# A one-hot of the expert gates moved from VectorE to ScalarE, in the first dense stage of a PEER layer

## The reference, cut to what matters

```python
sc, ci = lax.top_k(cand, PEER_TOPK)
e1 = jnp.take_along_axis(i1, ci // PEER_TOPK, axis=-1)
e2 = jnp.take_along_axis(i2, ci % PEER_TOPK, axis=-1)
idx = (e1 * N_KEYS + e2).reshape(PEER_BLOCK, PEER_HEADS * PEER_TOPK)
gate = jax.nn.softmax(sc, axis=-1).reshape(PEER_BLOCK, PEER_HEADS * PEER_TOPK)
u = lp['peer_u'][idx]
act = jax.nn.gelu(jnp.einsum('bkd,bd->bk', u, xb).astype(jnp.float32), approximate=False)
return jnp.einsum('bk,bkd->bd', (gate * act).astype(xb.dtype), lp['peer_v'][idx])
```

## Time and profile before

| | |
|---|---|
| time, median of 3 runs | 4661.38 us (4657.36 to 4670.94) |
| the profiled execution's own time | 4685.36 us |
| its span, first to last instruction | 4683.5 us |
| busy, share of the span | PE 77%, DVE 52%, POOL 32%, ACT 20% |
| mean granted clock of TensorE | 0.88 |

### The profile page before, as it was taken

One profiled execution on the slowest core, in us unless ns is written; L12 is line 12 of the kernel. 1 busy time (PEld: TensorE's weight loads), 2 busy tenths in 40 slices (PEclk: granted clock), 3 DMA queues, 4 the chain that ended last, 5 costly groups with the idle time before them and its releaser, 6 DMA issues. The chain is left out here.

```text
span 4683.5 us, 57981 instructions
## 1 busy us (share of the span) xinstructions
PE 3621.7 (77%) x21974; PEld 2555.1 (55%) x21974; DVE 2433.7 (52%) x5117; ACT 926.4 (20%) x1361; POOL 1483.9 (32%) x1266
## 2 busy tenths in 40 slices
PE   8687899985869969677878798764577677678894
PEld 2354576753546859566666575542344445444473
DVE  3055222225214330577879788789566566543354
ACT  1222111111222031122222232211111111111221
POOL 0000111100000112044555354557566566554400
PEclk9898899996979979888989899886788889889996
DMA  5200110111013052277889798788999999999963
GB/s 222 100 28 14 32 31 29 38 34 62 27 67 127 27 172 91 94 251 267 299 319 362 272 363 288 289 305 311 332 354 373 355 369 374 351 355 341 327 170 126
DMA packets 422161, 977.69 MB, mean 209 GB/s; under 512 B 164657, under 2 KB 191481, under 8 KB 417936
## 3 DMA queue, kind: packets, MB, share of 16 engines
q0 software_dynamic: 150912, 549.52, 31.5%
q1 hardware_dynamic: 270992, 424.63, 27.0%
HBM read 861.15 MB, written 112.88 MB: 208 GB/s over the span
## 5 line engine op out<-in xcount | busy, mean ns | idle before, releaser
L1874 POOL DMA_INDIRECT u_rows<-in_u_rows,idx_u x512 | 666.6, 1302 | 932.7 <-DVE dots L1912 687.4
L1885 POOL DMA_INDIRECT v_rows<-in_v,idx_v x512 | 631.9, 1234 | 312.5 <-PE ff_ps L1971 167.4
L1912 DVE CUSTOM_DVE_ANT_0 u_rows<-u_rows,x_rows 128x1024 f32<-128x1024 f32 x512 | 619.6, 1221 | 161.1 <-DMA u_rows<-in_u_rows,idx_u 135.2
L2306 PE MATMUL hid_ps<-dh,u_high 128*128 128x512 f32 x1024 | 427.8, 418 | 93.3 <-DVE u_low L2558 92.9
L2306 PE MATMUL hid_ps<-dl,u_high 128*128 128x512 f32 x1024 | 422.9, 413 | 0.0
L2306 PE MATMUL hid_ps<-dh,u_low 128*128 128x512 f32 x1024 | 420.8, 411 | 0.0
L2723 PE MATMUL turn_ps<-w_high,dh 128*128 128x512 f32 x384 | 170.5, 444 | 290.6 <-DVEq L2775 256.9
L1971 PE MATMUL ff_ps<-v_rows,diag 128*8 128x512 f32 x2048 | 264.9, 638 | 84.9 <-DMA v_rows<-in_v,idx_v 83.8
L2306 PEld LDWEIGHTS hid_ps<-dh,u_high 128*128 128x128 f32 x1024 | 202.6, 198 | 158.6 <-DVE u_low L2558 113.1
L2723 PEld LDWEIGHTS turn_ps<-w_high,dh 128*128 128x128 f32 x384 | 77.4, 201 | 358.4 <-DVEq L2775 204.6
L684 PE MATMUL side_ps_scan<-h,w_side_scan 128*128 128x344 f32 x768 | 269.1, 476 | 0.2
(11 more groups left out here) (407 smaller groups left out, 6780.1 us busy)
## 6 DMA issues: line engine op xcount, KB each, us to landing
u_raw<-in_u SPq DMA_DIRECT2D x128, 512.0 KB, 6.5
v_raw<-in_v SPq DMA_DIRECT2D x128, 512.0 KB, 5.9
hidden_saved<-hid SPq DMA_DIRECT2D x128, 256.0 KB, 5.9
gates_saved<-gates SPq DMA_DIRECT2D x64, 512.0 KB, 6.9
g_back<-gates_saved SPq DMA_DIRECT2D x16, 2048.0 KB, 39.8
hidden_back<-hidden_saved SPq DMA_DIRECT2D x128, 256.0 KB, 5.0
slab<-in_w_ada SPq DMA_DIRECT2D x12, 2048.0 KB
side_saved<-side_scan SPq DMA_DIRECT2D x16, 516.0 KB
```

The source lines that it names most:

```text
L1874: self.nc.gpsimd.indirect_dma_start(self.u[:, n % RU], None, self.io["u_rows"], bass.IndirectOffsetOnAxis(ap=index, axis=axis)).then_inc(l ...
L1885: self.nc.gpsimd.indirect_dma_start(self.v[:, n % RV], None, self.io["v"], bass.IndirectOffsetOnAxis(ap=index, axis=0)).then_inc(self.v_la ...
L1912: V.tensor_tensor_reduce(self.u[:, n % RU], self.u[:, n % RU], self.xt[:], 1.0, 0.0, ALU.mult, ALU.add, accum_out=self.dots[:, i % 2, k:k ...
L2306: mm = nc.tensor.matmul(ps[b % 2][:], u[:, b % 2, k], h[:, k], start=at == 0, stop=at == 3 * KD - 1)
```

## The change

`second` is no longer formed by DVE. ACT forms it: for each of the four tokens of a group one 128 x 128 activation Abs(index - key), with the index as a per-partition bias and scale -1, then, after a wait for its own four results, one 128 x 512 Relu(1 - x) in place, with a column of ones as bias. For integers this is 1 where they are equal and 0 elsewhere. ACT waits, as DVE does, until PE has used the buffer two groups before. The copy of the products out of PSUM becomes a list entry of its own, `take_gates`, placed behind the *next* group's `gates`; the store by SP goes with it. The planner counts a `gates` group as 1.6 in place of 2.3, and `take_gates` as nothing.

```diff
         if not kind.sparse:
-            groups = [("gates", kind.i * NGRP + g) for g in range(NGRP)]
+            groups = [(what, kind.i * NGRP + g - late) for g in range(NGRP + 1)
+                      for what, late in (("gates", 0), ("take_gates", 1)) if 0 <= g - late < NGRP]
...
-        else:
-            now += 2.3
+        elif item[0] == "gates":
+            now += 1.6
             pe += 1.1
...
-                    elif e[0] == "gates" and e[1] % 2 == 1:
+                    elif e[0] == "take_gates" and e[1] % 2 == 1:
                         b = e[1] // 2
                         sp.wait_ge(g_taken, e[1] + 1)
                         sp.dma_start(io["gates"][:, b], gates[:, b % 2]).then_inc(g_stored[b % 2], 16)
...
                         if kind.i >= 2:
-                            act.wait_ge(second_ready, (kind.i - 1) * NGRP)
+                            act.wait_ge(first_ready, (kind.i - 1) * NGRP)
+                            act.wait_ge(away, (kind.i - 1) * P)
...
                     elif e[0] == "gates":
+                        g = e[1]
+                        d = g // NGRP
+                        if g >= 2:
+                            act.wait_ge(g_summed, g - 1)
+                        if g % NGRP == 0:
+                            turn = next(k.m for k in SELECT if not k.sparse and k.i == d)
+                            act.wait_ge(s_taken, fills["turn", turn] + 1)
+                        for t in range(GRP):
+                            at = g % NGRP * GRP + t
+                            S.activation(second[:, g % 2, t], col(consts, "iota"), ACT.Abs, scale=-1.0,
+                                         bias=slots[:, d % 2, 1, at:at + 1]).then_inc(away, 1)
+                        act.wait_ge(away, (g + 1) * GRP)
+                        S.activation(second[:, g % 2], second[:, g % 2], ACT.Relu, scale=-1.0, bias=col(consts, "ones"))\
+                            .then_inc(second_ready, 1)
+                    elif e[0] == "take_gates":
                         g = e[1]
                         b = g // 2
                         act.wait_ge(g_summed, g + 1)
...
                         ins.then_inc(first_ready, 1)
-                        at = g % NGRP * GRP
-                        V.tensor_tensor(second[:, g % 2], iota.unsqueeze(1).to_broadcast([P, GRP, NKEY]),
-                                        slots[:, d % 2, 1, at:at + GRP].unsqueeze(2).to_broadcast([P, GRP, NKEY]),
-                                        ALU.is_equal).then_inc(second_ready, 1)
```

More of the change, by code:

```diff
@@ L2237, in peer_up @@
         (keys_loaded, u0, u1, u_high, u_low, summed, finished, h0, h1, q_loaded, scored, s_taken, read, chain, exp_in,
-         gate_ready, slots_ready, turned, first_ready, second_ready, g_summed, g_taken, g0_stored, g1_stored, up_carried) = sems(
+         gate_ready, slots_ready, turned, first_ready, second_ready, g_summed, g_taken, g0_stored, g1_stored, away, up_carried) = sems(
             ph, "keys_loaded", "u0_loaded", "u1_loaded", "u_high_ready", "u_low_ready", "hid_summed", "hid_finished",
             "hid0_stored", "hid1_stored", "q_loaded", "peer_scored", "s_taken", "s_read", "select_chain", "exp_in", "gate_ready",
-            "slots_ready", "slots_turned", "first_ready", "second_ready", "gates_summed", "gates_taken", "gates0_stored", "gates1_stored",
+            "slots_ready", "slots_turned", "first_ready", "second_ready", "gates_summed", "gates_taken", "gates0_stored", "gates1_stored", "second_away",
             "up_carried")
```

## The result

The changed kernel takes 4686.87 us (median of 8 runs), the one before 4664.48 in the same comparison: a ratio of 1.0049, 95% interval 1.0031 to 1.0067, so 22 us slower. One of the eight executions of the kernel before took 7797 us; without it the median before is 4661.38. The forecast was 17 us slower.

What follows compares the result with a forecast made beforehand. Peer_up was taken as bound mostly by PE, its tail by DVE, peer_down by transfers while gathers run. Peer_up 35 us shorter (44 - 16 + 7) and peer_down 52 longer gave +17: 4678 us on the median, range 4610 to 4725.

Steps and rivals of the forecast that it cites:

- The sum: Whole kernel: peer_up 35 us shorter and peer_down 52 longer, so 17 us slower.
- ACT's price: Gates groups: four Abs, a Relu, a short wait and the copy take 2.47 us of ACT, 79 us per set.
- The sets: Gates of D0 to D2: ACT becomes the pace, 119, 96, 102 us become 93, 90, 90; D3 gains 7.
- The tail: Stretch between the gates of D2 and D3: 13 blocks moved there bring their u_low onto full DVE, 16 us longer.
- peer_down: Second stage: 56 moved gathers add 115 us, dense pairs done beside them save 63 at the end; net 52 longer.
- ACT hidden: Rival, gates sets: ACT under about 1.9 us a group, sets go at PE's pace; 57 us faster, 4604; chance 0.22.
- Taking turns: Rival, gates sets: ACT's copy waits for PE and the next `second` for the copy; 140 us slower, 4801; chance 0.12.
- Table loads: Rival, Gelus among the gates of D0 to D2: two loads more each, 41 us on ACT; 4719; chance 0.04.

Runs made afterwards that it cites:

- e6: The changed kernel with one 128x512 Abs per group in place of four 128x128, three quarters of the one-hots wrong: 4656.35 us, ratio 0.9972.
- e3: The changed kernel with the planner's interval of gathers in peer_up at 2.1 in place of 2.3: 4678.13 us, ratio 1.0024.
- e7: The kernel before with the planner's gates cost at 1.6 and gather interval at 2.1, both one-hots on VectorE: 4663.5 us, ratio 0.9993.
- e1: The changed kernel with the planner's cost of a gates group put back from 1.6 to 2.3: 4689 us, ratio 1.0043.
- e2: The kernel before with the planner's cost of a gates group at 1.6 in place of 2.3, one-hot on VectorE: 4646.56 us, ratio 0.9948.
- e9: The kernel before with only the planner's gates cost at 1.6, measured again on one chip with three others: 4649.86 us, ratio 0.9963.
- e12: The changed kernel itself, measured again on one chip with three others: 4688.7 us, ratio 1.0037.
- e10: The changed kernel, plan and later copy kept, with the second one-hot back on VectorE, measured again on one chip: 4651.71 us, ratio 0.9960.
- e4: The kernel before with only the planner's interval of gathers in peer_up raised from 2.3 to 2.5: 4693.7 us, ratio 1.0054.
- e5: The changed kernel with ScalarE forming the second one-hot of even groups only, VectorE that of odd groups: 4670.06 us, ratio 1.0005.

## Why the prediction was right

**The sum.** Forecast: peer_up 35 us shorter, peer_down 52 longer, +17. Profiles: 47 shorter and 56 longer, with a long profile of before; +22 by the medians.

**ACT's price** was estimated at 0.39 us for an Abs, 0.71 for a Relu and 2.47 for a group: 0.390, 0.723 and 2.40. The nearest row, an activation with the same kind of operand, gave it to 3%. That ACT would be the pace of the gates sets was right for D1 to D3, 91 to 96% busy: e6 shows it, for nothing but ACT's work was shortened there. For D0, 84% busy, it was wrong, as e6 shows too.

**The sets.** Forecast 93, 90, 90 and 82 us; measured 103, 88, 84 and 77. D0 was the one too short: ACT has 86.6 of its 103 us, and the DMA engines are at 0.95. I had priced D0 by ACT alone. What holds it was not tried; with the gathers spread as in e3 and e7 it is 89 and 85 us. That the four come to 355 as forecast and 352 as measured is luck in part, for D0's 10 us make up for the 2, 6 and 5 of the others.

**The tail**: forecast 16 us longer for 13 `u_low`; 19 (121 to 140 us between the sets). The pieces moved as said: 178, 114 and 113 matmuls of L2307 in D0 to D2 in place of 278, 214 and 206, 37 pieces where I had said 40.

```profile
2372.00:2475.00 103.00, 50.39 (x178) 34.74 (x178) 0.95 0.95 345
2675.00:2763.00 88.00, 31.24 (x114) 21.22 (x115) 0.98 0.92 325
2960.00:3044.00 84.00, 29.58 (x113) 20.10 (x113) 1.00 0.87 309
```

The other 18 us of the 47 lie in the stretches between the sets, 8 before D0, 6 and 5 in the two selections. e1, with the old plan, has 452, 203 and 201 us there where before has 459, 206 and 202, so about half of the 18 is the long profile of before.

**peer_down**: 54 gathers moved, for 56 forecast, at 2.12 us each, and the part without gathers gave 60 back (117 us to 57); net 56.

**Where the account fell short** is its balance: it set the moved gathers against the relief of the gates sets, as if the first were the loss and the second the gain of the move to ScalarE. The runs show that the relief comes from the plan, and that the move to ScalarE is itself the loss. The shorter plan, gathers moved and all, is worth -17 to -24 us with the one-hot on VectorE (e2, e9). Taking the one-hot to ScalarE costs 37 us under that plan (e12 against e10), 20 under the old one (e1) and 15 with the shorter interval (e3 against e7). The moved gathers by themselves have no one price: under the old plan they cost 25 us (e4), under the shorter plan they are worth 14 to 21 with the one-hot on VectorE (e2 and e9 against e7) and cost 6 to 12 with it on ScalarE (e12 and the change against e3, by ratios whose intervals overlap). Why their sign changes was not tested. Peer_up gets part of the 52 us back, and that gain had no term in my sum except where a gates set was the place. The total came out because the sets were costed at ACT's pace, which already holds the loss: 355 us forecast and 352 measured, where the sets of e10, with the same plan and the one-hot on VectorE, are 318.

**The rivals.** *ACT hidden* did not come, and its price was wrong too: with ACT's work cut to some 1.8 us a group (e6, 57.5 us for the 32 of D3) the time is 4656, and not the 4604 that I had worked out from PE's pace; the sets stay at 69 to 79 us. *Taking turns* would fit e1, mildly (D1 10 us longer), but is not shown. *Table loads* did not come: the 128 + 512 new activations run without one, as the Trainium skill (ScalarE: Activation LUTs, Table sets: the hidden batching unit) says of relu and abs.

**A version below both kernels** is the plan alone, e2 and e9: 0.9948 and 0.9963 of the kernel before, one number changed in the planner. DVE's group takes 1.63 us there, and the planner now counts 1.6.

## What to carry to other kernels

Before work is moved to an idle engine, add up what that engine will spend on one turn of the loop it joins, copies included, and compare it with the turn of the engine that leads now: 2.4 us against 1.6 made an engine that was 30% busy the slowest in three of four sets. Where a planner's cost is changed together with the work, run the two apart: here the number in the planner gained 17 to 24 us and the moved work lost 37. And price work that shifts between two stages in both of them.

## What was not expected of the hardware

With half of the one-hots on ScalarE (e5), PE waited 52 us for an engine that was itself waiting 74 us for stores to land: it seems that the place behind a waiting copy, on an engine that takes its list in order, mattered more there than the load, though no run moved the copy. And the stretch of peer_down with gathers took 2.08 to 2.14 us for each gather of 512 KB in every profile, dense work beside it included, with the DMA engines at 0.98 to 1.01.
